# Attention step of an encoder layer: transposes, low halves and high halves each moved to the head of the step

## The reference, cut to what matters

```python
def one_block(qblk):
    s = jnp.einsum('bqhgd,bkhd->bhgqk', qblk, k).astype(jnp.float32) * scale
    p = jax.nn.softmax(s, axis=-1)
    return jnp.einsum('bhgqk,bkhd->bqhgd', p.astype(v.dtype), v)
```

## Time and profile before

| | |
|---|---|
| median of 3 runs | 3203.1 us (3201.27 to 3205.05) |
| profiled execution | 3203.52 us |
| its span, first to last instruction | 3201.7 us |
| granted TensorE clock, mean over the span | 0.983 |
| PE busy | 3086.6 us, 96% of the span |
| PEld, DVE, ACT, POOL busy | 82%, 56%, 45%, 13% |
| first and last transpose of probabilities (L715) | start at 282.4 and 693.8 us |

### The profile page before, as it was taken

How to read it: one execution, slowest core, us unless ns; L and a number is a source line. 1 busy time by engine, 2 the same in 40 slices (tenths; PEclk the granted TensorE clock), 3 DMA queues, 4 the chain that set the end, 5 groups by cost and what they waited for, 6 DMA issues and landing times.

```text
span 3201.7 us, 43742 instructions
## 1 busy us (share of the span) xinstructions
PE 3086.6 (96%) x15912; PEld 2612.5 (82%) x15912; DVE 1804.2 (56%) x1880; ACT 1446.9 (45%) x1807; POOL 417.4 (13%) x373
## 2 busy tenths in 40 slices
PE   7998999999976999999999999999999999999996
PEld 6997998978865888888888888888888888888885
DVE  6545887875665554545445455554545545455468
ACT  3225887871123444444444444444444444444464
POOL 2544241311122000000000000000000000001000
PEclk9998999999988999999999999999999999999998
DMA  6331010112245566565656656566565656656575
GB/s 210 124 107 52 11 31 25 40 54 112 114 147 173 181 213 189 205 210 183 211 185 212 213 187 210 181 212 202 191 211 182 214 188 211 211 182 212 183 262 211
DMA packets 371531, 532.71 MB, mean 166 GB/s; under 512 B 36720, under 2 KB 311920, under 8 KB 371440
## 3 DMA queue, kind: packets, MB, share of 16 engines
q1 hardware_dynamic: 356560, 488.50, 45.1%
q0 software_dynamic: 10656, 38.80, 4.7%
q10 hardware_dynamic: 4224, 4.19, 0.4%
HBM read 470.62 MB, written 60.82 MB: 166 GB/s over the span
## 4 chain that ended last, share of the span: by engine, by line
PE 86%; issue 5%; DVE 3%; POOLq 2%; POOL 1%; ACT 1%; DMA 1%; DVEq 1%; ACTq 0%; SPq 0%
PE ps_gu L902 43%; PE ps_y L940 20%; PE ps_o L790 6%; PE ps_pv L726 4%; PE ps_t L715 4%; PE ps_s L680 2%; PE ps_s L681 2%; PE ps_x L916 2%; PE ps_m L735 1%; PE ps_x L879 1%; POOLq L1664 1%; POOLq L1672 1%; PE ps_l L807 1%; POOL qkv L1678 1%; PE ps_m L666 0%
## 5 line engine op out<-in xcount | busy, mean ns | idle before, releaser
L1521 DVE TENSOR_TENSOR w_l<-w_raw,w_h 128x2048 fp32r<-128x2048 f32 x380 | 871.1, 2292 | 783.7 <-ACT w_h L1180 783.7
L1180 ACT ACTIVATE w_h<-w_raw 128x2048 fp32r<-128x2048 f32 x384 | 734.4, 1912 | 583.4 <-PE ps_gu L902 369.3
L902 PE MATMUL ps_gu<-w_h,x_h 128*128 128x512 f32 x2048 | 809.5, 395 | 0.0
L902 PE MATMUL ps_gu<-w_h,x_l 128*128 128x512 f32 x2048 | 799.7, 390 | 0.0
L902 PE MATMUL ps_gu<-w_l,x_h 128*128 128x512 f32 x2048 | 798.9, 390 | 0.0
L902 PEld LDWEIGHTS ps_gu<-w_h,x_l 128*128 128x128 f32 x2048 | 384.8, 188 | 81.3
L902 PEld LDWEIGHTS ps_gu<-w_l,x_h 128*128 128x128 f32 x2048 | 385.5, 188 | 76.2
L902 PEld LDWEIGHTS ps_gu<-w_h,x_h 128*128 128x128 f32 x2048 | 385.1, 188 | 76.4 <-DVE hf L1602 0.2
L940 PE MATMUL ps_y<-w_h,hh 128*128 128x512 f32 x1024 | 323.2, 397 | 0.0
L940 PE MATMUL ps_y<-w_l,hh 128*128 128x512 f32 x1024 | 316.7, 391 | 0.0
L940 PE MATMUL ps_y<-w_h,hl 128*128 128x512 f32 x1024 | 316.3, 390 | 0.0
(11 more groups left out here) (254 smaller groups left out, 3997.4 us busy)
## 6 DMA issues: line engine op xcount, KB each, us to landing
w_raw<-in_w_gate SPq DMA_DIRECT2D x256, 512.0 KB, 3.6
w_raw<-in_w_up SPq DMA_DIRECT2D x256, 512.0 KB, 4.7
w_raw<-in_w_down SPq DMA_DIRECT2D x128, 1024.0 KB, 4.9
xin<-in_x SPq DMA_DIRECT2D x16, 512.0 KB, 5.7
xln_d<-xln SPq DMA_DIRECT2D x16, 512.0 KB, 5.2
res<-xln_d SPq DMA_DIRECT2D x16, 512.0 KB, 3.2
h_d<-hid SPq DMA_DIRECT2D x16, 512.0 KB, 2.7
acc_d<-acc SPq DMA_DIRECT2D x16, 512.0 KB, 2.6
```

The lines of the kernel that those rows point to most:

```text
L902: last = nc.tensor.matmul(out_gu, a[:, k, tok], w[:, kk, :], start=k == 0 and q == 0, stop=k == KD - 1 and q == 2)
L1180: nc.scalar.activation(w_h[:, c % RING, :], w_raw[:, c % RING, :], ACT.Copy).then_inc(w_hi, 1)
L1521: nc.vector.tensor_tensor(w_l[:, c % RING, :], w_raw[:, c % RING, :], w_h[:, c % RING, :].bitcast(f32), ALU.subtract).then_inc(w_lo, 1)
```

## The change

Within a step, three engines get another order. PE: the transposes of t come ahead of the scores of t+2 and of the turned blocks. ACT: the high halves of t come ahead of the turned blocks; the exponential of t+2 stays last. DVE: the low halves of t come ahead of the maximum of t+2. No instruction, wait or buffer is added or taken away.

```diff
@@ PE, stage_b @@
                     if t < NSTEP:
+                        transposes(t)
                         if t + 2 < NSTEP:
                             scores(s, t + 2, here, False, q_turn(s, first, last_s, (t + 2) // GT))
                         elif not last_s:
...
                         for what in before_step(t, last_s):
                             ahead = what[0] == "K" or what[1] == 0
                             through_m(turn_no(s, last_s, what), what, s + 1 if ahead else s)
-                        transposes(t)
                     pv, add, bk = after_step(t, first)
@@ ACT, stage_b @@
                     if t < NSTEP:
+                        hi(t)
                         for what in before_step(t, last_s):
                             from_m(turn_no(s, last_s, what), what, there)
-                        hi(t)
                         if t + 2 < NSTEP:
                             exp(s, t + 2, False)
@@ DVE, stage_b @@
                     if t < NSTEP:
+                        lo(t)
                         if t + 2 < NSTEP:
                             row_max(s, t + 2)
                         elif not last_s:
                             row_max(s + 1, t + 2 - NSTEP)
-                        lo(t)
                         if t == 1 and not first:
                             v_lo_sub(s)
```

## The result

| | before | after |
|---|---|---|
| median, us (lowest to highest, 4 runs each) | 3202.18 (3201.02 to 3205.05) | 3358.12 (3357.34 to 3359.47) |
| ratio, 95% interval | | 1.0486 [1.0468, 1.0504] |
| profiled run, us (its span) | 3203.5 | 3357.34 (3355.5) |
| first high half to high half of step 126, us | 406.83 | 562.24 |
| clock granted to TensorE in the stage | 0.99 | 0.91 |

The account below looks back on a forecast made before the run. PE was taken to bound the attention stage. 563.5 us for the new order less 406.8 gives +156.7; with -1.5, -1.1 and +2 it is +156.1, on 3203.5: 3360 us, range 3343 to 3400.

Parts of the forecast that it names:

- The ring: Attention stage: ACT and DVE take turns through four start-to-start hops, 4.27 us a step against 3.23; 126 times, 538.0 us.
- The unknown hops: ACT, exponential to high half and copy to high half: 1.11 and 0.26 us taken; upper ends add 7.6 and 10.0 us.
- The edge of the loop: Where slot 1 ends: ACT and DVE may pause at the loop body's edge; +2 us, bounds nothing and 10.9 us.
- The ends: Attention stage's two ends: first high half at 282.43 instead of 283.90, -1.5 us; last step some 2.0 instead of 3.09, -1.1 us.
- costs nothing in this: ACT's order: the turned block sits between high halves and exponential, where ACT would be idle; no cost.
- were never what ACT will wait for: PE's order: transposes come earlier, but ACT could begin at 1.9 us of 4.27, so no effect on time.
- should read 1.00 but for the slot's edge: PE's clock in the attention stage: expected to stay at 1.00, with PE busy about 72%.
- first rival: Attention stage: PE's clock falls as well, every second pair of steps cold, 125 us more, 3485 us; chance 8%.
- The waits: Attention stage: DVE's low halves wait for ACT, ACT's exponentials for maxima, some 200 us each; PE waits for low halves.

Follow-up runs that it names:

- The split low halves: The changed kernel, but VectorE takes the maximum between the two low halves of a step instead of behind both: 3282.04 us, ratio 1.0251.

## Why the prediction was right, point by point

- **The ring.** Forecast 0.63 + 1.20 + 1.33 + 1.11 = 4.27 us; measured 0.63 + 1.21 + 1.33 + 1.10 = 4.27, in slot 1, from which all four hops had been taken. The stage took 562.24 us; 563.5, and 2 for the loop's edge, were forecast. That it came so close is in part luck: the 62 passes in slots 0 and 3 are some 0.08 us shorter each, 5 us in all, and five other passes in the loop's slots are 0.3 to 0.6 us longer than the ring says, 2 us in all. Neither was foreseen. The split low halves confirm it: taking 0.60 us out of the ring gave back 126 times that, within 1 us.
- **The unknown hops.** The lower ends were right to take: with no wait for PE mixed in, exponential to high half is 1.10 (not 1.23) and copy to high half 0.26 (not 0.37).
- **The edge of the loop.** 2 us taken between bounds of 0 and 10.9. From the exponential at 564.95 to the high half at 567.90 it is 2.95 us instead of 1.10: 1.85 more. The high half waited 1.74 us there for PE, whose timeline shows a pause like that of the earlier trace rows, and behind it transposes of 1.96 us instead of the 1.06 of the earlier trace rows:

```profile
565.79 1.96 PE L715 MATMUL ps_t<-ident,prob 128*128 128x128 f32 x8 [3.19 <-issue]
```

So what came through was PE's pause, not one of ACT's own, for which the 2 us had been set.

- **The ends.** First high half at 282.25 (282.43 forecast), last step 2.12 us (2.0). The 1.1 us that the sum took off for the last step do not show in the total, though: behind step 126 the two kernels take the same time.
- **ACT's edit "costs nothing in this"**: true in the change as a whole, where the block lies in a pause (there are 42 blocks; the 48 of the prediction is an upper bound). As a statement on the edit it is too wide: alone it costs 60 us, and with VectorE's edit alone 15 more.
- **PE's transposes "were never what ACT will wait for"**: true with the transposes first, but for the loop's edge, and only then. With PE in the order of before the high halves waited 47.4 us for them. The edit was needed to keep PE out of the ring; the prediction counted it as neutral because it looked only at the order after. The number came out right as that is the order the change has.
- **The clock "should read 1.00 but for the slot's edge": wrong.** It read 0.91. The prediction leaned on 8 us at the end of the stage, in which PE was about 76% busy at 1.00; that was too short a stretch to speak for 560 us. By its own test (0.5 to 0.9 means that the first rival holds) the reading stood at the rival's edge, and the test was badly made: here the clock fell without PE being what binds. More and less work for PE showed that the time doesn't hang on it. The Trainium skill, "TensorE: Matmul & The Clock Gate", section "A second HAM failure mode: psum-queue depth-cycling", says that short idles between groups of matmuls can make the clock swing. This trace agrees (0.83 and 1.00 in neighbouring stretches of 10 us). The 125 us that the prediction put on this rival did not come.
- **The waits** of DVE and ACT were forecast at some 200 us each: 227.1 and 237.2. PE was to wait for low halves; its transposes did so for 14.3 us only, and it waited longer, 34.6 us, to add halves behind the turned query blocks.

## What to carry to other kernels

When engines run in order, look in a new order for a closed chain of waits from one step to the next, add up its hops as start-to-start times from the trace, and set the sum against the bound engine's work per step: the longer of the two is the new pace, and rings don't add. What an edit is worth hangs on the order of the other engines: TensorE's lost 139 us alone and saved 50 beside the two others. A maximum, a load or any other work that needs nothing of this step should stand ahead of work that does; one such swap on an engine that had a fifth of its time to spare cost 191 us here. A falling clock or a lower busy share of the engine that used to bind is often only a mark of waiting: give that engine more work, and see whether the time moves, before counting it as a cost. With all three edits it cost nothing; with TensorE's alone, where PE was in the chain, 13.6 us.

## What the runs showed of the hardware

- In the kernel after, TensorE's clock fell to 0.83 in some stretches of 10 us and to 0.91 in the mean of the stage, and came back to 1.00 in others, with PE busy about 80% in both kinds (8.20 and 8.07 of 10 us). 59 us more of matmuls, spread over 128 steps, put the mean at 0.99.
- Redundant matmuls can make a kernel faster: 13.6 us, where PE is in the chain and the filling held the clock at 0.99 instead of 0.96.
- Two low halves, each 686 ns long, and the maximum behind them start 0.60 us apart: the split maximum gained 0.60 a step, not 0.69. A hop has to be taken from starts, not from durations.
